# Head norm, output projection and feed-forward norm: three stages, or one stage in four phases

## The reference

```python
o_a = hgrn2_mixer(...)      # 4 heads of 64: head_rmsnorm(o, norm_w) * silu(g)
o_b = rglru_mixer(...)      # width 512
o_c = gla_mixer(...)        # 4 heads of 64: head_rmsnorm(o, norm_w) * silu(g)
x = x + jnp.concatenate([o_a, o_b, o_c], axis=-1) @ w_out[l]
h = rmsnorm(x, norm_ffn[l])
gate = causal_dwconv(h @ ffn_w_gate[l], ffn_conv_w[l], ffn_conv_b[l])
x = x + (jax.nn.gelu(gate) * (h @ ffn_w_val[l])) @ ffn_w_down[l]
```

## Time and profile before

| | us |
|---|---|
| runs | 3317.78, 3316.55, 3314.16 (median 3316.55) |
| profiled execution | 3316.03, of which span 3314.4 |
| TensorE busy, share of the span | 2960.5, 89% |
| VectorE, ScalarE, GpSimd | 1642.8 (50%), 1040.2 (31%), 709.4 (21%) |
| mean TensorE clock | 0.938 |

### The profile page before, as it was taken

The page is one execution under the profiler, slowest core; times in us unless marked ns, Lnnn a source line. Parts: engine busy times, 40 slices in busy tenths (PEclk is TensorE's granted clock), DMA queues, the critical chain, the costliest instruction groups (busy, mean ns, idle before and its releaser), DMA issues. The chain is left out here.

```text
span 3314.4 us, 38950 instructions
## 1 busy us (share of the span) xinstructions
PE 2960.5 (89%) x14684; PEld 2348.8 (71%) x14684; DVE 1642.8 (50%) x2813; ACT 1040.2 (31%) x2087; POOL 709.4 (21%) x454
## 2 busy tenths in 40 slices
PE   6999675969999999959998999998799998999988
PEld 4768575438888888848767787776677676877766
DVE  4170785023313323323578753485535787633865
ACT  3151553021001000020367342174103673421751
POOL 1233010003333233313111301402141113014021
PEclk8999776979999999979999999998899999999989
DMA  3001001111021111123012001204230120012032
GB/s 107 33 32 38 1 1 55 51 38 49 32 68 45 35 61 45 39 95 85 11 47 79 16 1 62 66 1 138 85 108 19 45 74 23 1 52 76 1 127 89
DMA packets 78799, 168.36 MB, mean 51 GB/s; under 512 B 14848, under 2 KB 33808, under 8 KB 78096
## 3 DMA queue, kind: packets, MB, share of 16 engines
q1 hardware_dynamic: 70160, 140.61, 12.7%
q10 hardware_dynamic: 8448, 25.18, 2.8%
HBM read 128.00 MB, written 20.97 MB: 45 GB/s over the span
## 5 line engine op out<-in xcount | busy, mean ns | idle before, releaser
L296 PE MATMUL psum<-H,ffn_W 128*128 128x512 f32 x672 | 262.8, 391 | 13.7 <-POOL ffn_W L1390 12.0
L298 PE MATMUL psum<-H,ffn_W 128*128 128x512 f32 x672 | 262.4, 390 | 0.0
L297 PE MATMUL psum<-H,ffn_W 128*128 128x512 f32 x672 | 262.4, 390 | 0.0
L1388 POOL CAST ffn_W<-ffn_W 128x1024 fp32r<-128x1024 f32 (+1 forms) x84 | 69.3, 825 | 676.8 <-PE psum L298 448.0
L1685 DVE TENSOR_SCALAR_CACHE_REDUCE MB<-OM,tk_mid 128x512 bf16<-128x512 f32 (+2 forms) x192 | 184.3, 1010 | 2.3
L1654 ACT ACTIVATE MB<-OM,tk_mid 128x384 bf16<-128x384 f32 (+2 forms) x192 | 157.0, 819 | 48.6 <-DVE tk_mid L1682 44.5
L482 POOL TENSOR_TENSOR tk_W<-tk_W 128x1024 fp32r<-128x1024 f32 (+1 forms) x38 | 79.9, 2106 | 423.1 <-ACT tk_W L434 423.1
L1464 DVE TENSOR_SCALAR ffn_Y<-ffn_G,ffn_par 128x1024 f32<-128x1024 f32 x21 | 22.2, 1058 | 298.6 <-ACT ffn_G L1453 298.6
L1390 POOL TENSOR_TENSOR ffn_W<-ffn_W 128x1024 fp32r<-128x1024 f32 (+1 forms) x84 | 161.4, 1922 | 6.7
L296 PEld LDWEIGHTS psum<-H,ffn_W 128*128 128x128 f32 x672 | 126.8, 189 | 41.1 <-POOL ffn_W L1390 12.2
L297 PEld LDWEIGHTS psum<-H,ffn_W 128*128 128x128 f32 x672 | 126.8, 189 | 26.4
(11 more groups left out here) (420 smaller groups left out, 7609.8 us busy)
## 6 DMA issues: line engine op xcount, KB each, us to landing
OM<-in_w_feat SPq DMA_DIRECT2D x34, 512.0 KB, 4.4
tk_W<-in_w_feat SPq DMA_DIRECT2D x22, 512.0 KB, 3.5
ffn_W<-in_ffn_w_gate SPq DMA_DIRECT2D x21, 512.0 KB, 3.4
ffn_W<-in_ffn_w_val SPq DMA_DIRECT2D x21, 512.0 KB, 3.4
ffn_W<-in_ffn_w_down SPq DMA_DIRECT2D x42, 256.0 KB, 2.7
OM<-MB ACTq DMA_DIRECT2D x64, 128.0 KB, 2.6
OM<-OM ACTq DMA_DIRECT2D x64, 128.0 KB, 3.0
fin_W<-in_w_out SPq DMA_DIRECT2D x4, 2048.0 KB, 11.2
```

Source lines behind the costliest of these rows:

```text
L296: pe.matmul(out, a1, b1, start=start, stop=False)
L297: pe.matmul(out, a1, b2, start=False, stop=False)
L298: return pe.matmul(out, a2, b1, start=False, stop=stop)
L1388: pool.tensor_copy(w1, w).then_inc(rounded, 1)
```

## The change

The three stages after the attention become one, `closing_stage`, with a helper `Closing` whose work stands at the end of `gla_stage`.

- In the attention's last pass SyncE loads the two column halves of the 4 weight blocks that belong to the recurrent part (`o_b`, stored in BG). ScalarE rounds one block of BG after the copy of O in each of chunks 3 to 6, in chunk 6 also one half of the weights, and in chunk 7 applies the two Silus. GpSimd subtracts to get the low parts.
- In `closing_stage` TensorE runs 4 phases of 8 row tiles: BG times columns 0 to 511, BG times columns 512 to 1023, then the head-normed O times each half. Each tile is 4 feature blocks of three products, into one of 4 PSUM banks, and VectorE adds it to X. All factors are split in a rounded and a low part.
- The head norm goes tile by tile beside phases 0 and 1; TensorE's transpositions of O stand after products 6 to 13, with two PSUM banks for them.
- The feed-forward's norm goes tile by tile in phase 3, each with its own root; TensorE turns tile t-1 after the products of tile t.
- X's rows are loaded tile by tile; the idle products are gone. Buffers share addresses with others that are no longer in use.

```diff
@@ gla_stage: SyncE, GpSimd after its last memset, ScalarE after the copy of O @@
+                sp.wait_ge(mixed, 2 * len(pass_of))
+                closing.load(sp)
...
+                closing.lows(pool)
...
+                        if p == NP - 1 and c >= 3:
+                            closing.beside_last_pass(act, c - 3)
...
@@ head_norm_stage and residual_stage are replaced @@
+class Closing:
...
+    def load(self, sp):
+        for c in range(2):
+            sp.dma_start(self.raw[c].rearrange("p (k n) -> p k n", k=4),
+                         self.w_view[:, 2:6, c * HALF:(c + 1) * HALF]).then_inc(self.weights_in, 16)
+        sp.wait_ge(self.weights_in, 32)
+    def beside_last_pass(self, act, n):
+        if n < 4:
+            act.activation(self.BG_high[:, n, :], self.BG[:, n, :], ACT.Copy).then_inc(self.bg_high, 1)
+        if n == 3:
+            act.wait_ge(self.weights_in, 32)
+            act.activation(self.parts[2], self.raw[0], ACT.Copy).then_inc(self.weights_high, 1)
+        if n == 4:
+            for V in (self.VA, self.VC):
+                act.activation(V[:, :, 256:512], V[:, :, 256:512], ACT.Silu).then_inc(self.gated, 1)
+    def lows(self, pool):
+        for n in range(4):
+            pool.wait_ge(self.bg_high, n + 1)
+            pool.tensor_tensor(self.BG_low[:, n, :], self.BG[:, n, :], self.BG_high[:, n, :].bitcast(FP32),
+                               ALU.subtract).then_inc(self.bg_low, 1)
+            pool.wait_ge(self.bg_low, n + 1)
+        pool.wait_ge(self.weights_high, 1)
+        pool.tensor_tensor(self.parts[0], self.raw[0], self.parts[2].bitcast(FP32), ALU.subtract
+                           ).then_inc(self.weights_low, 1)
+        pool.wait_ge(self.weights_low, 1)
+def closing_stage(kit, closing, O, O_rounded, VA_rounded, gains, X, x_in, H1, H2, F1, GF, gain_ffn, ident):
...
+    BG_W = [(b2, b0), (piece(0), b1)]
+    OT_W = [(piece(2), piece(1)), (b0, b2)]
...
+                for t in range(NT):
+                    sp.dma_start(X[:, t, :], x_in[t * P:(t + 1) * P, :]).then_inc(x_ready[t], 16)
+                for c in range(2):
+                    if c:
+                        sp.wait_ge(products, NT)
+                    to = four(OT_raw[c][1])
+                    at = slice(c * HALF, (c + 1) * HALF)
+                    sp.dma_start(to[:, 0:2, :], closing.w_view[:, 0:2, at]).then_inc((ot_in0, ot_in1)[c], 16)
+                    sp.dma_start(to[:, 2:4, :], closing.w_view[:, 6:8, at]).then_inc((ot_in0, ot_in1)[c], 16)
...
+            def _(pool):
+                pool.wait_ge(w_high, 1)
+                pool.tensor_tensor(b1, r1, piece(0).bitcast(FP32), ALU.subtract).then_inc(w_low, 1)
+                for c in range(2):
+                    high, low = OT_W[c][0].bitcast(FP32), OT_raw[c][1]
+                    pool.wait_ge(w_low, c + 1)
+                    pool.wait_ge(w_high, c + 2)
+                    pool.tensor_tensor(OT_W[c][1], low, high, ALU.subtract
+                                       ).then_inc(w_low, 1)
...
+                act.wait_ge(sums, NT + 1)
+                act.activation(ss, ss, ACT.Sqrt, scale=1.0 / 64, bias=eps_col).then_inc(root, 1)
+                act.activation(piece(0), r1, ACT.Copy).then_inc(w_high, 1)
+                act.wait_ge(ot_in0, 32)
+                act.activation(OT_W[0][0], OT_raw[0][1], ACT.Copy).then_inc(w_high, 1)
+                for t in range(NT):
+                    act.wait_ge(turned, t + 1)
+                    act.activation(O_rounded[:, t, :], kit.psum[:, t % 2, :], ACT.Copy).then_inc(ot_high, 1)
+                act.wait_ge(products, NT)
+                act.wait_ge(ot_in1, 32)
+                act.activation(OT_W[1][0], OT_raw[1][1], ACT.Copy).then_inc(w_high, 1)
+                for t in range(NT + 1):
+                    if t < NT:
+                        act.wait_ge(added, LAST + t + 1)
+                        act.activation(junk, X[:, t, :], ACT.Square, accum_out=sumsq[:, t:t + 1]).then_inc(squared, 1)
+                        act.wait_ge(squared, t + 1)
+                        act.activation(inv[:, t:t + 1], sumsq[:, t:t + 1], ACT.Sqrt, scale=1.0 / D, bias=eps_col
+                                       ).then_inc(ln_root, 1)
+                    if t:
+                        act.wait_ge(ln_turned, t)
+                        act.activation(H1[:, :, (t - 1) * P:t * P],
+                                       kit.pair((t - 1) % 2).rearrange("p (k n) -> p k n", k=KT), ACT.Copy
+                                       ).then_inc(copied, 1)
...
+                def add(m):
+                    c, t = (m // NT) % 2, m % NT
+                    if m < NT:
+                        dve.wait_ge(x_ready[t], 16)
+                    dve.wait_ge(products, m + 1)
+                    if m >= NT:
+                        dve.wait_ge(added, m - NT + 1)
+                    x = X[:, t, c * HALF:(c + 1) * HALF]
+                    dve.tensor_tensor(x, x, kit.psum[:, 4 + m % 4, :], ALU.add).then_inc(added, 1)
+                def gate(t):
+                    o = O[:, t, :].rearrange("p (h w) -> p h w", h=H)
+                    own.then(dve.tensor_tensor(o, o, ss[:, t, :].unsqueeze(2).to_broadcast([P, H, 64]), ALU.mult))
+                    own.then(dve.tensor_tensor(O[:, t, :], O[:, t, :], G, ALU.mult))
+                    dve.tensor_tensor(O[:, t, 0:256], O[:, t, 0:256], VA[:, t, 256:512], ALU.mult)
+                    dve.tensor_tensor(O[:, t, 256:512], O[:, t, 256:512], VC[:, t, 256:512], ALU.mult).then_inc(rows, 1)
...
+                def norm(t):
+                    dve.wait_ge(ln_root, t + 1)
+                    own.then(dve.reciprocal(inv[:, t:t + 1], inv[:, t:t + 1]))
+                    if t >= 2:
+                        dve.wait_ge(ln_turned, t - 1)
+                    dve.scalar_tensor_tensor(ROWS[:, t % 2, :], X[:, t, :], inv[:, t:t + 1], GF, ALU.mult, ALU.mult
+                                             ).then_inc(normed, 1)
...
+                dve.sem_inc(sums, 1)
+                for m in range(3):
+                    add(m)
+                dve.wait_ge(gain_in, 32)
+                dve.wait_ge(root, 1)
+                own.then(dve.reciprocal(ss, ss))
+                for m in range(3, LAST):
+                    if m - 3 < NT:
+                        gate(m - 3)
+                    add(m)
+                    if 7 <= m < 7 + NT:
+                        low(m - 7)
+                dve.wait_ge(gf_in, 16)
+                for t in range(NT + 2):
+                    if t < NT:
+                        add(LAST + t)
+                    if 1 <= t <= NT:
+                        norm(t - 1)
+                    if t >= 2:
+                        part(t - 2)
...
+                def turn(t):
+                    pe.wait_ge(rows, t + 1)
+                    if t >= 2:
+                        pe.wait_ge(ot_low, t - 1)
+                    for k in range(K4):
+                        last = pe.transpose(kit.psum[:, t % 2, k * P:(k + 1) * P], O[:, t, k * P:(k + 1) * P], ident)
+                    last.then_inc(turned, 1)
+                def turn_norm(t):
+                    pe.wait_ge(normed, t + 1)
+                    if t >= 2:
+                        pe.wait_ge(parted, t - 1)
+                    for k in range(KT):
+                        last = pe.transpose(kit.pair(t % 2)[:, k * P:(k + 1) * P], ROWS[:, t % 2, k * P:(k + 1) * P],
+                                            ident)
+                    last.then_inc(ln_turned, 1)
+                for m in range(4 * NT):
+                    phase, t = divmod(m, NT)
+                    if phase and t == 0:
+                        pe.wait_ge(w_low, phase)
+                    if phase == 2:
+                        pe.wait_ge(ot_low, t + 1)
+                    if m >= 4:
+                        pe.wait_ge(added, m - 3)
+                    at = slice(t * P, (t + 1) * P)
+                    high, low = (four(a) for a in (BG_W, OT_W)[phase // 2][phase % 2])
+                    for k in range(K4):
+                        a1, a2 = (BG_high[:, k, at], BG_low[:, k, at]) if phase < 2 else (OT_high[:, t, k, :],
+                                                                                          OT_low[:, t, k, :])
+                        last = three_products(pe, kit.psum[:, 4 + m % 4, :], a1, a2, high[:, k, :], low[:, k, :],
+                                              k == 0, k == K4 - 1)
+                    last.then_inc(products, 1)
+                    if 6 <= m < 6 + NT:
+                        turn(m - 6)
+                    if phase == 3 and t:
+                        turn_norm(t - 1)
+                turn_norm(NT - 1)
...
@@ first_block @@
-        head_norm_stage(kit, "hn", OM, ...)
-        residual_stage(kit, "wout", tiles, ...)
-    norm_stage(kit, "ffnnorm", X, H1, ident, d["norm_ffn"], rest=H2)
+        closing = Closing(kit, BG, BG_high, BG_low, WB, WB_rounded, VA, VC, d["w_out"])
```

(2 more changed lines are left out.)

215 lines of the change are left out of this document (93 added, 122 removed).

## The result

| | before | changed |
|---|---|---|
| runs beside each other, us | 3314.16 to 3318.82, median 3317.16 (4 runs) | 3260.36 to 3265.29, median 3263.18 (4 runs) |
| ratio | | 0.9844, 95% interval 0.9831 to 0.9856 |
| span of the profiled execution | 3314.4 | 3263.5 |

The account below looks back on a forecast made before the run. It took three stages chained end to end, 541.1 to 733.8 (192.7 us), as the whole field. Its terms put the feed-forward's start at 689.1, 44.7 us earlier: 3316.0 - 44.7 = 3271.3, or 3271.9 from the median, taken as 3272; range 3255 to 3286.

Parts of the forecast that it names:

- the likeliest case: The whole sum as forecast, 3272 us, with its own band 3266 to 3278; chance 0.48.
- the clock in phase 3: TensorE at half rate for about 3.5 us after each of seven waits, losing 1.75 each, 12.3 us; bounds 0 to 25.
- stall with its clock: TensorE waits 6.6 us before the third head transposition for the first low part, plus 1.8 of low clock: 8.4.
- rival A: The clock holds in phase 3's short waits; 12.3 us and part of the stall's 1.8 go: 3258; chance 0.17.
- The second clock step: After the stall at the third head transposition TensorE's clock is low again, costing 1.8 us.
- GpSimd and VectorE: In the stage, two GpSimd subtractions of 4.7 us, at about 557 and 568.5, hold up VectorE's gating; they take turns.
- Rival B: VectorE and GpSimd don't meet, as subtractions fall between gatings or the banks cover them: 3264; chance 0.18.
- Rival C: The last attention pass slows, GpSimd's four BG subtractions each holding the chunk chain for 2.34 us: 3281; chance 0.11.
- D: The clock stays low through the whole stage, as late VectorE keeps opening small waits: 3346; chance 0.03.
- E: A wait, the late weights' rounding, holds phase 3 and adds some 5 us; 2%, or 0.03 with the rest.
- The block's end: The last attention pass ends at 546.9, 5.8 us later, after a table load and two Silus of 3.7 together.
- The product's term: 128 fp32 products filling 110 us are replaced by 384 with rounded operands at 0.226 us each, 86.7 us.

Follow-up runs that it names:

- e2: The changed kernel with four PSUM banks in turn instead of two for the transpositions of the head-normed tiles; 3257.16 us, ratio 0.9832.
- e3: The changed kernel with GpSimd's three 128x2048 subtractions in the new stage replaced by fills with zero, which read nothing from SBUF; 3255.26 us, ratio 0.9827.
- e10: The changed kernel with the two Silus moved from the last attention pass back into the stage, on ScalarE after the roots; 3266.62 us, ratio 0.9856.
- e7: The changed kernel with ScalarE squaring each tile of phase 3 twice; 3264.07 us, ratio 0.9855.
- e12: The changed kernel with GpSimd's three 128x2048 subtractions in the stage cut into 8 pieces of 128x256 each; 3265.19 us, ratio 0.9855.
- e4: The changed kernel with one fp32 matmul of the rounded factors in place of three products of parts; 3273.23 us, ratio 0.9881.
- e6: The changed kernel with two idle fp32 products of 128x512 before each phase 3 wait for the normed tile; 3257.11 us, ratio 0.9831.

## Why the prediction was right, point by point

Each wait was where it was put, and no rival came whole. The time, 3263, lies 9 us under the forecast and 3 outside the likeliest case's own 3266 to 3278: one term of the sum, the clock in phase 3, was too large by as much. The misses of the other terms (products 2.8 more, and the norm's transpositions 1.5, at 6.05 - 2.17 - 2.80 = 1.08 for 0.86 each; waits 2.0, stall with its clock 1.5 and start at the low clock 1.0 less) nearly cancel, and that is luck.

| step | forecast | measured |
|---|---|---|
| last copy of O | 0.8 late | 0.75 (541.57 for 540.82), 0.52 of it its own |
| stage starts | 547.2 | 547.48 |
| start at the low clock | 2.6 | 1.6 (1.00 from 550.7) |
| tile of 12 products | 2.71 | 2.80 (0.233 a product) |
| stall at the third head transposition, with clock | 6.6 + 1.8 | 4.3 + 2.6 |
| phase 3 begins | 626.6 | 626.7 |
| seven waits | 7 x 2.46 = 17.2 | 7 x 2.17 = 15.2 |
| clock in phase 3 | 12.3 | 3.2 |
| feed-forward starts | 689.1 | 680.81 |

- **The mis-sized term is the clock in phase 3.** The step was: waits of this size put the clock down each time, from two waits of 2.71 and 2.65 us. The waits were 2.17 us, between those and the 1.78 at which it had held, and it fell in two of seven; in six periods of the same waits the traces show two falls with the change, e2, e3 and e10, four with e7 and e12, none with e4. e6 prices all of it at 3.4 us. So rival A, to which I gave 0.17, is nearer to what was measured on this point than the forecast, and its 3258 lies 5 us below the median, my 3272 lies 9 above. The Trainium skill (TensorE: Matmul & The Clock Gate, "HAM oscillation") shows a new fall in each tile for waits longer than these. The trace agrees in that five of the seven waits of 2.17 us brought no fall; the other two brought one, so shorter waits can lower the clock too, though not each time.
- **The second clock step, at the stall, was too small**: 2.6 for 1.8, because the clock stayed low for 5 us behind it.
- **GpSimd and VectorE** met as worked out: subtractions from 556.46 and 568.83 for "about 557" and "about 568.5", 4.61 for 4.7. The second met the gating of tile 3, not of tile 2, since tile 0's gating ended at 563.1 for 563.9 and each further one with its add took 2.72 for 2.85; so the first low part was there at 579.4 instead of 581.7, and the stall was 4.3 instead of 6.6. e3 shows that the subtractions are the cause, e2 that the two banks are the way. The Trainium skill (SBUF — State Buffer, section "Who interferes with whom") says that a VectorE instruction with two SBUF inputs and a GpSimd one that reads SBUF exclude each other; e12 agrees, and shows that it is for one instruction at a time (no VectorE operation above 1.12 us beside pieces of GpSimd's work). Rival B is false.
- **Rival C** (the attention pass slows): chunks stayed at 3.48 us (535.16 to 538.64, before 534.93 to 538.41), so GpSimd's subtractions cost the chain of a chunk nothing. **D** and **E** are false: 0.95 and 0.90 of clock, and no wait for weights at phase 3. The 60% at which D was said to cross the kernel before is a slip: by its own terms it is (44.7 + 16.7 + 6.6) / 96.9, 70%.
- **The block's end** at 546.9 was right by a cause I had named second: I had given it to the Silus, "GpSimd's last subtraction not the later one by much". e10 shows that without the Silus it is no earlier.
- **The product's term** was right in what it removes and adds (110 for 86.7, measured 89.5) and says little of the gain: by e4 it is 11 of 53, because the faster product uncovers VectorE's lateness and the clock's falls.
- A gain of 53.0 in the stage and 1.1 up to the feed-forward's first product (8.2 for 9.3 us) stand beside 54 in the median. The profiled execution, the slowest of its four at 3265.29, shows 3 us less in the span (50.9), within what the untouched rest varies.

## What to carry to other kernels

Read a wait inside an interleaved loop from the order on the engine that ends it: here two operations in the wrong order on VectorE cost 16 us, and even without the interleaving the kernel was 6 faster. Where two engines share a resource and one gets late, look for the buffer count that hands this on; a second pair of banks was worth as much as removing the conflict. A clock term read from two waits is an upper bound, not a price for each of seven.

## What the runs showed of the hardware that was not expected

- Equal waits of 2.17 us lowered TensorE's clock in some cases and not in others: in the first six of each trace twice with the change, e2, e3 and e10, four times with e7 and e12, and never with the fp32 products of e4. No run tells why. A fall cost 1.6 us where a tile's products followed. At the seventh wait, behind which only the last transposition is left, it fell with e2, e3, e7 and e10 and held in the other three. Two idle products of 0.86 us in each wait kept it at 1.00.
- Beside a GpSimd subtraction of two SBUF operands, VectorE's multiplications of two SBUF operands wait (2.66 and 4.90 for 0.68 us), while its adds of an SBUF and a PSUM operand (0.69 at 557.76) and its reciprocal do not. In both cases the subtraction was under way first; where a VectorE multiplication was (568.69 to 569.37 in e10), the subtraction issued at 568.84 took 5.01 for 4.61. In pieces, both slow: 1.11 for 0.69 us, and 8.11 for the 5.62 of the same pieces with no gating beside them.
- The same products stood 0.233 us apart in this stage, and 0.226 in the feed-forward; no run here tells why.
- The rest of the program, unchanged in 14 kernels, took 2566.2 to 2576.1 us, so one profiled execution says nothing of 5 us outside the stage that is looked at.
